# Recurrence steps: two of the four gate tiles behind s are placed between u and the outputs

## The reference

```
proj = h @ w_in                      # its last 4096 columns are gate_mla, gate_rwkv
def step(st, inp):                   # st: one 64 x 64 state per direction and head
    sa = einsum('dbhij,dbhj->dbhi', st, a_t)
    st = st * w_t + sa * b_t + v_t * k_t
    y  = einsum('dbhij,dbhj->dbhi', st, r_t)
merged = sigmoid(gate_mla) * u_mla + sigmoid(gate_rwkv) * u_rwkv
```

## Time and profile before

| | |
|---|---|
| median of 3 runs | 3397.88 us |
| the runs | 3392.94 to 3399.22 us |
| the profiled execution, its own time | 3389.71 us |
| its span, first to last instruction | 3388.4 us |
| TensorE busy over the span | 96% |
| VectorE, ScalarE busy over the span | 67%, 45% |
| the 8 pairs of the recurrence | about 420 to 843 us of the span |

### The profile page before, as it was taken

One profiled execution on the slowest core, in us unless ns is written; L12 is line 12 of the kernel. 1 busy time (PEld: TensorE's weight loads), 2 busy tenths in 40 slices (PEclk: granted clock), 3 DMA queues, 4 the chain that ended last, 5 costly groups with the idle time before them and its releaser, 6 DMA issues.

```text
span 3388.4 us, 71888 instructions
## 1 busy us (share of the span) xinstructions
PE 3255.3 (96%) x30322; PEld 3103.4 (92%) x30322; DVE 2275.4 (67%) x2978; ACT 1517.0 (45%) x1835; POOL 74.3 (2%) x154
## 2 busy tenths in 40 slices
PE   8999899999998999999999999999989999999998
PEld 8998888888898769999999999989879899999998
DVE  8776856565687977777655544565656777777545
ACT  5442454443244035544444343453454555545443
POOL 0000100000000000000000000000000000000000
PEclk9999999999999999999999999999999999999999
DMA  8758723232786544677655555534424455555554
GB/s 322 261 204 329 273 86 107 86 108 92 279 346 238 187 161 175 252 290 283 240 190 194 193 195 198 187 127 165 159 100 163 162 191 192 186 187 193 190 197 152
DMA packets 94146, 664.19 MB, mean 196 GB/s; under 512 B 10353, under 2 KB 10993, under 8 KB 15346
## 3 DMA queue, kind: packets, MB, share of 16 engines
q1 hardware_dynamic: 74736, 540.05, 44.4%
q0 software_dynamic: 14400, 104.86, 8.0%
q10 hardware_dynamic: 4802, 16.12, 1.2%
HBM read 654.70 MB, written 6.29 MB: 195 GB/s over the span
## 4 chain that ended last, share of the span: by engine, by line
PE 86%; DVE 9%; ACT 2%; issue 1%; DMA 1%; ACTq 0%; SPq 0%; DVEq 0%
PE ps L463 22%; PE ps L462 22%; PE ps L464 21%; PE ps L434 4%; PE ps L657 4%; PE ps L641 2%; PE ps L493 2%; PE ps L642 2%; PE ps L643 2%; DVE ring_parts L1837 2%; DVE work L1860 1%; DVE work L2113 1%; PE ps L506 1%; DVE ring_parts L1845 1%; PE ps L650 1%
## 5 line engine op out<-in xcount | busy, mean ns | idle before, releaser
L1837 DVE TENSOR_TENSOR ring_parts<-ring,ring_hi 128x1024 fp32r<-128x1024 f32 x866 | 1042.1, 1223 | 701.2 <-ACT ring_hi L1158 687.3
L1158 ACT ACTIVATE ring_hi<-ring 128x1024 fp32r<-128x1024 f32 x866 | 909.4, 1059 | 1141.6 <-PE ps L464 1094.9
L463 PE MATMUL ps<-h_lo,ring_hi 128*128 128x256 f32 x2624 | 729.2, 278 | 0.0
L462 PE MATMUL ps<-h_hi,ring_hi 128*128 128x256 f32 x2112 | 593.1, 281 | 15.8 <-DVE h_lo L1867 8.5
L464 PE MATMUL ps<-h_hi,ring_parts 128*128 128x256 f32 x2112 | 585.1, 277 | 0.0
L463 PEld LDWEIGHTS ps<-h_lo,ring_hi 128*128 128x128 f32 x2624 | 497.7, 190 | 1.4 <-issue 1.2
L462 PE MATMUL ps<-x_hi,ring_hi 128*128 128x256 f32 x1664 | 466.3, 280 | 9.7 <-DVE x_lo L1867 5.8
L463 PE MATMUL ps<-x_lo,ring_hi 128*128 128x256 f32 x1664 | 462.9, 278 | 0.0
L464 PE MATMUL ps<-x_hi,ring_parts 128*128 128x256 f32 x1664 | 461.0, 277 | 0.0
L462 PEld LDWEIGHTS ps<-h_hi,ring_hi 128*128 128x128 f32 x2112 | 397.0, 188 | 18.2 <-issue 9.8
L464 PEld LDWEIGHTS ps<-h_hi,ring_parts 128*128 128x128 f32 x2112 | 397.0, 188 | 0.0
(11 more groups left out here) (471 smaller groups left out, 5781.3 us busy)
## 6 DMA issues: line engine op xcount, KB each, us to landing
ring<-in_weights SPq DMA_DIRECT2D x511, 1024.0 KB, 4.8
work<-in_ada POOLq DMA_DIRECT2D x96, 1024.0 KB, 6.7
work<-in_c_row POOLq DMA_DIRECT2D x4, 1024.0 KB, 5.6
gate_store<-gate_out ACTq DMA_DIRECT2D x8, 512.0 KB, 6.2
work<-gate_store ACTq DMA_DIRECT2D x2, 2048.0 KB, 19.4
resid<-in_lora ACTq DMA_DIRECT2D x9, 256.0 KB, 5.4
resid<-in_x SPq DMA_DIRECT2D x4, 512.0 KB, 6.0
resid<-in_x ACTq DMA_DIRECT2D x1, 2048.0 KB, 28.0
```

The source lines that it names most:

```text
L462: mm(o, w_hi[:, k, cols], hi(kc), start=(kc == 0 and m % 2 == 0), stop=False, skip_group_check=True)
L463: mm(o, w_hi[:, k, cols], lo(kc), start=False, stop=False, skip_group_check=True)
L1158: A(high_ring(n)[:, 2 * (e % 2) + half, :], ring[:, n % RING, half * (SLOT // 2):(half + 1) * (SLOT // 2)], ACT.Copy)\
L1837: tt(lo, x, high_ring(n)[:, e % 4, :].bitcast(F32), ALU.subtract).then_inc(S("lo_ready"), 1)
```

## The change

In steps 1 to 3, two gate tiles are issued between the products of u and the outputs, by `gate_tiles(34 + 8 * k, 2, i)`; these are tiles 42 and 43, 50 and 51, 58 and 59. They are taken from the block of four behind s of the step before, `gate_tiles(40 + 8 * k, ...)`, which now issues two. The order of the 64 tiles among themselves is the same, and so are all waits and reports.

```
@@ -775,6 +775,7 @@
                     gate_tiles(32, 4, i)
                     t.wait(S("xy_ready"), 2)
                 else:
+                    gate_tiles(34 + 8 * k, 2, i)
                     for d in range(2):
                         for hs in HALVES:
                             product(y(hs, chunk[d]), ST[hs, d, :], AR[hs, 4 * d + chunk[d], 1, :], start=(k == 1 and d == 0))
@@ -794,7 +795,7 @@
                             ins = mm(PS[hs, 3 + 3 * d, CH:2 * CH], BKT[:, e, h * CH:(h + 1) * CH], SV[:, e, h, :],
                                      start=True, stop=True)
                         t.give(ins, S("s_mm"))
-                    gate_tiles(40 + 8 * k, 4, i)
+                    gate_tiles(40 + 8 * k, 2, i)
```

## The result

The changed kernel took 3416.17 us in the median of 9 runs (3403.49 to 3428.95), the kernel before 3397.91 us (3392.94 to 3410.54): the ratio is 1.0039, with a 95% interval of 1.0022 to 1.0057. (The quotient of the two medians alone is 1.0054, within that interval.) It is slower, as forecast; the forecast 1.0025 lies near the lower end of the interval.

A forecast was written before the change was run, and what follows sets the result against it. TensorE's own order was taken to bound the steps; 0.20 + 0.16 = 0.36 us a step over 24 steps made 8.6 us, added to the 3397.88 median: 3406.5 us (0.25% more), range 3399.0 to 3412.0.

The forecast's parts named there:

- The bound: In the steps, TensorE's own order sets the pace; the waits list names no copy of u and no state.
- The u wait, the gain at nothing: Before sa, outputs already cover the copies of u by about 0.07 us; gain nothing, at most 1.7 us in all.
- The cover of s: Six gate matmuls behind s instead of twelve still cover DVE's state, with 0.27 us in hand a step; cost nothing.
- The price of the cut: Each step pays 0.20 us for one more gate-run beginning plus 0.16 for parting u from yS; 8.6 us in all.
- The rival of the cheaper cut: In the steps, yS loses nothing heading a run: 0.20 us a step, 4.8 us in all, 3402.7 us; chance 0.20.
- The estimate from the Trainium skill: Two more shape changes a step, each draining TensorE about 128 cycles: 0.11 us a step, 2.6 in all, 3400.5 us.
- The issue waits: Rival: PE's 11.0 us of issue waits in small-product runs shrink, giving the loss back; no change or faster; chance 0.12.
- the spread of a measurement: Scatter of the whole kernel's measured time around the forecast sum, giving the forecast's own range, 3402 to 3410 us.

The follow-up runs named there:

- at_shape: Edit of the changed kernel: the two tiles stand between yS and yV, not between u and yS; steps 145.35 us, 4.9 over before, ratio 1.0019.
- two_cuts: Against the kernel before: one tile between u and yS, one between yS and yV; steps 153.95 us, 13.5 over before, ratio 1.0037.
- u_bare: Against the kernel before: tiles unmoved, outputs put behind sa so nothing covers the copies of u; steps 153.33 us, 12.9 over, ratio 1.0028.
- one_tile: Edit of the changed kernel: one tile moved, not two, leaving three behind s; steps 149.13 us, 8.7 over before, ratio 1.0025.
- all_four: Against the kernel before: all four tiles between u and the outputs, none behind s; steps 159.55 us, 19.1 over before, ratio 1.0057.

## Why the prediction was right, and where it was not

**The bound.** Right: TensorE's own order set the length of the steps, and it still does. A step of 2.78 us became one of 3.13.

**The u wait, the gain at nothing.** Right, and no longer an inference: 0.81 us wanted, 0.88 there.

**The cover of s.** Right: with two tiles the loads of u begin 0.30 to 0.44 us after the state is done, in all 24 steps of each of the three profiles. With no tile they begin 0.05 us after it, which is the handover, and TensorE waits 0.56 us a step. So two tiles leave at least 0.25 us in hand, where 0.27 was forecast.

**The price of the cut.** 0.20 for a beginning measured 0.20; 0.16 for u from yS measured 0.15; 0.36 a step measured 0.35 to 0.36; 8.6 us in all measured 8.5. The choice of 0.16 over 0 was made on single rows, and four ways to cut gave the prices that follow from them. The rival of the cheaper cut is refuted. A nearer rival is one price for each change of shape that a cut adds (the weights have 64x64, 128x64 or 128x128): one in at_shape, two in the changed kernel, three in two_cuts. By the 4.9 us of the first it would make 9.8 and 14.7 us; 8.5 and 13.5 were measured. What holds up the first matmul of a run, no run shows. The estimate from the Trainium skill ("TensorEngine Tiling (Array Packing)", Key Properties; "TensorE: Matmul & The Clock Gate", "Step-by-step: what each phase is for"), a drain for each change of shape, made 0.11 us a step. 0.35 was measured, so a drain at that price is not enough; whether it is a part of the 0.35 is not shown.

**The issue waits.** They gave nothing back: 11.0 us before and 13.5 in its second profile; 11.9, 12.7 and 12.6 in the three of the changed kernel.

**What was missed.** The mechanism and the sum were right; too small was what the prediction calls "the spread of a measurement", 3402 to 3410 us around its 3406.5. The three ratios of the changed kernel are 1.0039, 1.0018 and 1.0030; the steps account for 8.5 us, 1.0025. The rest is the executions' doing, so how near the total came to the forecast is in part luck. The first median, 3416.17 us, lies above the range's 3412. In its profiled execution (3416.92 us) the last stretch went at the slower pace. That pace costs 6191 x 2.2 ns = 14 us there, or 6694 x 2.2 ns = 15 us in the middle stretch. Six of the 9 executions, this one among them, lie some 10 us or more above the lower three (3403.5 to 3405.9). For the other five the same reason is likely but not shown, since only this one was profiled. It was not foreseen since one profile showed one pace only; the runs before the forecast had a spread of 6 us.

**What stays open.** Whether the change has a part in how often the slower pace comes. No profile of the kernel before shows it in a long stretch (two profiles); of the eight profiles of the other kernels six do, all but two_cuts and u_bare. By the times, which hold other scatter too, 25 of 91 executions of the kernel before (all its runs here together) lay at or above 3405 us. With this bound shifted by what each kernel's steps cost, there were 17 of 33 of the changed kernel, 4 of 12 of one_tile, 7 of 12 of at_shape, 2 of 10 of two_cuts, 4 of 10 of all_four and 1 of 10 of u_bare. That is 35 of 87 against 25 of 91; the changed kernel alone has half of its executions there, and one_tile, with the same steps to 0.2 us, a third. No run separates a kernel's own odds from chance, and I do not count the excess as the change's.

## What to carry to other kernels

Before filler work is put in front of a wait, look whether the wait sticks out from its cover; here 0.07 us of slack was to be read from three rows, and the filler could only cost. In these steps the number of runs counted, not the work in them: each cut of a run of large matmuls cost 0.20 us, with one tile moved as with two, and where it parted small products that overlapped, 0.15 us more. If a cut must be, try it first where the shape of the products changes anyway; here it was cheapest there. And where the time of a whole execution scatters by more than the change, measure the changed part itself: the 8.5 us of the steps came back within about 1 us in each profile of the changed kernel, while its ratio went from 1.0018 to 1.0039, by some 7 us.

## What the runs showed of the hardware

A long stretch of matmuls (128x128 weights, 256 columns, each with its weight load) goes at one of two paces, 115.6 or 117.8 ns a matmul, from its beginning to its end; the ten profiles show no third one in the three long stretches. It is not the granted clock, which is 1.00 in both. The two differ in rhythm: from each of the three lines `L462`, `L463`, `L464` to the next start there are 118.3, 115.8 and 112.5 ns at the faster pace, and 117.5, 117.5 and 118.3 ns at the slower (means of 2700 to 3300 us, before and after). The starts of the last stretch of before and of after look alike (timeline; start us, us, idle before):

```profile
2658.97 0.38 PE L462 MATMUL ps<-h_hi,ring_hi 128*128 128x256 f32 x1 [2.67 <-DVE ring_parts L1837]
2659.19 0.28 PE L463 MATMUL ps<-h_lo,ring_hi 128*128 128x256 f32 x1
2659.31 0.28 PE L464 MATMUL ps<-h_hi,ring_parts 128*128 128x256 f32 x1
```

```profile
2672.40 0.39 PE L462 MATMUL ps<-h_hi,ring_hi 128*128 128x256 f32 x1 [2.68 <-DVE ring_parts L1838]
2672.63 0.28 PE L463 MATMUL ps<-h_lo,ring_hi 128*128 128x256 f32 x1
2672.75 0.28 PE L464 MATMUL ps<-h_hi,ring_parts 128*128 128x256 f32 x1
```

Both begin behind a wait of 2.7 us, and the second stays 1.9% slower for 6191 matmuls. What decides it was not found. In this kernel the middle or the last stretch at the slower pace is worth 0.4% of an execution, more than the change itself, and both lie far behind the part that was changed.
